# Expert weight tables: one product a token in place of two, the other one-hots from another engine

## The reference

```
e1 = jnp.take_along_axis(i1, ci // K, axis=-1)
e2 = jnp.take_along_axis(i2, ci % K, axis=-1)
idx = e1 * PEER_NKEYS + e2
g = jax.nn.softmax(sc, axis=-1)
...
a = jnp.einsum('cd,chkd->chk', xc, u[ic])
act = (jax.nn.gelu(a.astype(jnp.float32)) * gc).astype(xc.dtype)
return jnp.einsum('chk,chkd->cd', act, v[ic])
```

## Time and profile before

| | us |
|---|---|
| median of 3 runs | 4493.68 (4482.83 to 4499.79) |
| the profiled execution | 4483.95 |
| its span | 4482.2 |
| stage `expert_weights`, steps with quads (64) | about 1234 to 1702 |
| the same stage, steps without (16) | about 1702 to 1793 |

### The profile page before, as it was taken

One profiled execution on the slowest core, in us unless ns is written; L12 is line 12 of the kernel. 1 busy time (PEld: TensorE's weight loads), 2 busy tenths in 40 slices (PEclk: granted clock), 3 DMA queues, 4 the chain that ended last, 5 costly groups with the idle time before them and its releaser, 6 DMA issues. The chain is left out here.

```text
span 4482.2 us, 49622 instructions
## 1 busy us (share of the span) xinstructions
PE 4152.0 (93%) x18593; PEld 3324.3 (74%) x18600; DVE 2397.5 (53%) x4975; ACT 1390.3 (31%) x2104; POOL 107.2 (2%) x84
## 2 busy tenths in 40 slices
PE   6987888699999999899999999898999899898998
PEld 5863676478888888788888776676888667776886
DVE  3236345559999993454444444565442444565443
ACT  2222233223344443232222232243222232243221
POOL 0003000000000000000000000100000001000000
PEclk8987878899999999999999998999999999999999
DMA  2214000233444444666666322232223222242222
GB/s 99 98 44 78 1 1 17 69 104 136 143 145 183 184 186 171 196 190 189 193 189 191 102 83 68 73 128 83 94 92 92 75 73 78 67 143 76 94 90 71
DMA packets 188675, 491.87 MB, mean 110 GB/s; under 512 B 19554, under 2 KB 61956, under 8 KB 187300
## 3 DMA queue, kind: packets, MB, share of 16 engines
q1 hardware_dynamic: 188452, 488.88, 33.8%
HBM read 407.02 MB, written 81.79 MB: 109 GB/s over the span
## 5 line engine op out<-in xcount | busy, mean ns | idle before, releaser
L1016 DVE TENSOR_TENSOR stream_lo<-stream_raw,stream_hi 128x1024 fp32r<-128x1024 f32 (+1 forms) x538 | 653.4, 1215 | 750.7 <-ACT stream_hi L1008 749.2
L1008 ACT ACTIVATE stream_hi<-stream_raw 128x1024 fp32r<-128x1024 f32 (+1 forms) x538 | 563.1, 1047 | 1269.0 <-PE experts_ps L1464 492.1
L1464 PE MATMUL experts_ps<-outputs_a_hi,stream_hi 128*128 128x512 f32 x1024 | 404.6, 395 | 14.3 <-DVE outputs_a_lo L1434 14.3
L1045 PE MATMUL experts_ps<-h_hi,stream_hi 128*128 128x512 f32 x1024 | 406.7, 397 | 5.9 <-DVE stream_lo L1016 4.4
L1045 PE MATMUL experts_ps<-h_lo,stream_hi 128*128 128x512 f32 x1024 | 402.6, 393 | 0.0
L1464 PE MATMUL experts_ps<-outputs_a_hi,stream_lo 128*128 128x512 f32 x1024 | 402.2, 393 | 0.0
L1045 PE MATMUL experts_ps<-h_hi,stream_lo 128*128 128x512 f32 x1024 | 400.0, 391 | 0.0
L1464 PE MATMUL experts_ps<-outputs_a_lo,stream_hi 128*128 128x512 f32 x1024 | 398.3, 389 | 0.0
L2341 PE MATMUL ffn_ps<-h_hi,stream_hi 128*128 128x512 f32 x704 | 287.6, 408 | 25.3 <-DVE h_lo L2378 25.3
L2341 PE MATMUL mid_ps<-h_hi,stream_hi 128*128 128x512 f32 x672 | 288.2, 429 | 23.8 <-DVE h_lo L2378 20.8
L2342 PE MATMUL ffn_ps<-h_lo,stream_hi 128*128 128x512 f32 x704 | 279.6, 397 | 0.0
(11 more groups left out here) (437 smaller groups left out, 7713.8 us busy)
## 6 DMA issues: line engine op xcount, KB each, us to landing
stream_raw<-u SPq DMA_DIRECT2D x128, 512.0 KB, 3.4
stream_raw<-v SPq DMA_DIRECT2D x128, 512.0 KB, 4.0
stream_raw<-l_gu SPq DMA_DIRECT2D x88, 512.0 KB, 3.2
expert_hidden<-experts_gelu SPq DMA_DIRECT2D x128, 256.0 KB, 2.3
expert_weights<-weights_built SPq DMA_DIRECT2D x8, 4096.0 KB, 14.5
outputs_wgt<-expert_weights SPq DMA_DIRECT2D x32, 1024.0 KB, 7.9
outputs_a_raw<-expert_hidden SPq DMA_DIRECT2D x128, 256.0 KB, 4.2
stream_raw<-l_gate SPq DMA_DIRECT2D x48, 512.0 KB, 3.6
```

The source lines that it names most:

```text
L1008: self.nc.scalar.activation(self.hi[n % self.RING][:, 0:w], self.raw[n % self.RAW][:, 0:w], ACT.Copy).then_inc(self.hi_done, 1)
L1016: self.nc.vector.tensor_tensor(self.lo[n % self.RING][:, 0:w], self.raw[n % self.RAW][:, 0:w], self.hi[n % self.RING][:, 0:w].bitcast(F32) ...
L1045: mm = self.nc.tensor.matmul(self.ps[n % 2], a, b[:, k, :], start=(k == 0 and m == 0), stop=(k == DC - 1 and m == 2))
L1464: mm = nc.tensor.matmul(ps[d], v, a[b % RING][:, :], start=(b == 0 and m == 0), stop=(b == KEYS - 1 and m == 2))
```

## The change

The roles of the three tiles are swapped. The one-hot of e1 is now plain, and ScalarE makes it: four instructions Abs(iota - e1) of 128 columns and one Relu(1 - x) of 512 columns in place, a quad (`ones`, `hot1`); `minus` holds -e1. The one-hot of e2 carries the weight, and VectorE makes both halves, times the rounded g and times its rest, in one scalar_tensor_tensor of 256 columns a token (`weighted`, `hot2`); g has rounded value and rest side by side. TensorE does one product of 256 columns a token, the e1 tile stationary, and so the two halves arrive in PSUM side by side and are not added there. VectorE adds them on the way out, in one tensor_reduce a quad that reads 1024 values a partition, a pair being 128 words apart, and writes 512 (`take`). A quad fills two PSUM banks, so three places take six banks. The 128 quads are spread over 72 of the 80 steps, one or two a step.

```
--- before.py
+++ after.py
@@ -1261,69 +1261,87 @@
-    QUAD, RING, BANKS, BUILT = 4, 3, 4, 2
+    QUAD, RING, PLACES, BUILT = 4, 3, 3, 2
     N = SEQ // QUAD
     TILE = WT // QUAD
     first, last = CHOICE_STEPS, KEYS
-    PER = 2
+    SPREAD = last - first - 8
     with Stage(nc, name) as st:
-        g_hi, g_lo = st.sb("g_hi", [P, SEQ], F32R), st.sb("g_lo", [P, SEQ])
-        hot = [st.sb(f"hot{b}", [P, QUAD, 3, KEYS], F32R) for b in range(RING)]
+        g, minus = st.sb("g", [P, SEQ, 2], F32R), st.sb("minus", [P, SEQ])
+        hot1 = [st.sb(f"hot1_{b}", [P, QUAD, KEYS], F32R) for b in range(RING)]
+        hot2 = [st.sb(f"hot2_{b}", [P, QUAD, 2, KEYS], F32R) for b in range(RING)]
         built = [st.sb(f"built{b}", [P, KEYS, WT]) for b in range(BUILT)]
-        g_hi_done, g_lo_done, hot_done, mm_done, taken = (
-            st.sem(x) for x in ("g_hi_done", "g_lo_done", "hot_done", "mm_done", "taken"))
+        minus_done, g_hi_done, g_lo_done, far_done, hot1_done, hot2_done, mm_done, taken = (
+            st.sem(x) for x in ("minus_done", "g_hi_done", "g_lo_done", "far_done", "hot1_done", "hot2_done", "mm_done", "taken"))
         stored = [st.sem(f"stored{b}") for b in range(BUILT)]
         def quads(n):
-            return range(max(0, min(N, PER * (n - first))), max(0, min(N, PER * (n - first + 1))))
+            done = [N * max(0, min(SPREAD, step)) // SPREAD for step in (n - first, n - first + 1)]
+            return range(*done)
+        def place(quad):
+            return ps[:, 1024 * (quad % PLACES):1024 * (quad % PLACES) + 1024].rearrange("p (t s e) -> p t s e", t=QUAD, s=2)
         with nc.Block() as block:
             @block.scalar
             def _(act):
-                nc.scalar.activation(g_hi[:, :], chosen[:, 2, :], ACT.Copy).then_inc(g_hi_done, 1)
-                def take(quad):
-                    tt = quad // TILE
-                    if tt >= BUILT and quad % TILE == 0:
-                        act.wait_ge(stored[tt % BUILT], 16 * (tt // BUILT))
-                    act.wait_ge(mm_done, quad + 1)
-                    at = quad % TILE * QUAD
-                    nc.scalar.activation(built[tt % BUILT][:, :, at:at + QUAD].rearrange("p e t -> p t e"),
-                                         ps[quad % BANKS].rearrange("p (t e) -> p t e", t=QUAD),
-                                         ACT.Copy).then_inc(taken, 1)
+                nc.scalar.activation(minus[:, :], chosen[:, 0, :], ACT.Copy, scale=-1.0).then_inc(minus_done, 1)
+                nc.scalar.activation(g[:, :, 0], chosen[:, 2, :], ACT.Copy).then_inc(g_hi_done, 1)
+                act.wait_ge(minus_done, 1)
+                def ones(quad):
+                    if quad >= RING:
+                        act.wait_ge(mm_done, quad - RING + 1)
+                    to = hot1[quad % RING]
+                    for k in range(QUAD):
+                        t = quad * QUAD + k
+                        ins = nc.scalar.activation(to[:, k, :], C.iota, ACT.Abs, bias=minus[:, t:t + 1])
+                    ins.then_inc(far_done, 1)
+                    act.wait_ge(far_done, quad + 1)
+                    nc.scalar.activation(flat(to[:, :, :]), flat(to[:, :, :]).bitcast(F32), ACT.Relu, bias=C.ones[:, 0:1],
+                                         scale=-1.0).then_inc(hot1_done, 1)
                 for n in range(first, last):
                     hidden.activate(act, n - 1)
                     chunks.high(act, n + AHEAD)
+                    for quad in quads(n):
+                        ones(quad)
+                hidden.activate(act, last - 1)
+            @block.vector
+            def _(dve):
+                V = nc.vector
+                dve.wait_ge(g_hi_done, 1)
+                V.tensor_tensor(g[:, :, 1], chosen[:, 2, :], g[:, :, 0].bitcast(F32), ALU.subtract).then_inc(g_lo_done, 1)
+                dve.wait_ge(g_lo_done, 1)
+                def weighted(quad):
+                    if quad >= RING:
+                        dve.wait_ge(mm_done, quad - RING + 1)
+                    both = [P, 2, KEYS]
+                    for k in range(QUAD):
+                        t = quad * QUAD + k
+                        ins = V.scalar_tensor_tensor(out=hot2[quad % RING][:, k, :, :], in0=C.iota.unsqueeze(1).to_broadcast(both),
+                                                     scalar=chosen[:, 1, t:t + 1],
+                                                     in1=g[:, t, :].bitcast(F32).unsqueeze(2).to_broadcast(both),
+                                                     op0=ALU.is_equal, op1=ALU.mult)
+                    ins.then_inc(hot2_done, 1)
+                def take(quad):
+                    tt, at = quad // TILE, quad % TILE * QUAD
+                    if tt >= BUILT and quad % TILE == 0:
+                        dve.wait_ge(stored[tt % BUILT], 16 * (tt // BUILT))
+                    dve.wait_ge(mm_done, quad + 1)
+                    V.tensor_reduce(built[tt % BUILT][:, :, at:at + QUAD].rearrange("p e t -> p t e"),
+                                    place(quad).rearrange("p t s e -> p t e s"), AX_X, ALU.add).then_inc(taken, 1)
+                for n in range(first, last):
                     for quad in quads(n - 1):
                         take(quad)
-                hidden.activate(act, last - 1)
-            @block.vector
-            def _(dve):
-                dve.wait_ge(g_hi_done, 1)
-                nc.vector.tensor_tensor(g_lo[:, :], chosen[:, 2, :], g_hi[:, :].bitcast(F32),
-                                        ALU.subtract).then_inc(g_lo_done, 1)
-                dve.wait_ge(g_lo_done, 1)
-                def ones(quad):
-                    if quad >= RING:
-                        dve.wait_ge(mm_done, quad - RING + 1)
-                    for k in range(QUAD):
-                        t = quad * QUAD + k
-                        key1, key2 = chosen[:, 0, t:t + 1], chosen[:, 1, t:t + 1]
-                        V = nc.vector
-                        V.tensor_scalar(hot[quad % RING][:, k, 0, :], C.iota, key1, g_hi[:, t:t + 1].bitcast(F32),
-                                        ALU.is_equal, ALU.mult)
-                        V.tensor_scalar(hot[quad % RING][:, k, 1, :], C.iota, key1, g_lo[:, t:t + 1],
-                                        ALU.is_equal, ALU.mult)
-                        ins = V.tensor_scalar(hot[quad % RING][:, k, 2, :], C.iota, key2, None, ALU.is_equal)
-                    ins.then_inc(hot_done, 1)
-                for n in range(first, last):
                     for quad in quads(n):
-                        ones(quad)
+                        weighted(quad)
                     chunks.low(dve, n + AHEAD)
             @block.tensor
@@ -1331,13 +1349,13 @@
                 for n in range(first, last):
                     hidden.product(pe, n)
                     for quad in quads(n):
-                        pe.wait_ge(hot_done, quad + 1)
-                        if quad >= BANKS:
-                            pe.wait_ge(taken, quad - BANKS + 1)
+                        pe.wait_ge(hot1_done, quad + 1)
+                        pe.wait_ge(hot2_done, quad + 1)
+                        if quad >= PLACES:
+                            pe.wait_ge(taken, quad - PLACES + 1)
                         for k in range(QUAD):
-                            out, of = ps[quad % BANKS][:, k * KEYS:(k + 1) * KEYS], hot[quad % RING]
-                            nc.tensor.matmul(out, of[:, k, 0, :], of[:, k, 2, :], start=True, stop=False)
-                            mm = nc.tensor.matmul(out, of[:, k, 1, :], of[:, k, 2, :], start=False, stop=True)
+                            mm = nc.tensor.matmul(place(quad)[:, k, :, :], hot1[quad % RING][:, k, :], hot2[quad % RING][:, k, :, :],
+                                                  start=True, stop=True)
                         mm.then_inc(mm_done, 1)
             @block.sync
@@ -2332,7 +2350,7 @@
                     hidden.ps = bank[0:2]
                     expert_choice(nc, "choice", C, q, A["subkeys"], chosen, chunks, hidden,
                                   ps[:, 1024:3072].rearrange("p (h k) -> p h k", k=KEYS), bank[6])
-                expert_weights(nc, "weights", C, chosen, w_dram, chunks, hidden, bank[2:6])
+                expert_weights(nc, "weights", C, chosen, w_dram, chunks, hidden, ps[:, 1024:4096])
             expert_outputs(nc, "outputs", x, w_dram, a_dram, chunks, bank, C2, A["positions"], constants2)
```

More of the change, by code:

```diff
@@ L1298, in _ @@
                     chunks.high(act, n + AHEAD)
-                    for quad in quads(n - 1):
-                        take(quad)
+                    for quad in quads(n):
+                        ones(quad)
                 hidden.activate(act, last - 1)
@@ L1324, in _ @@
                 for n in range(first, last):
+                    for quad in quads(n - 1):
+                        take(quad)
                     for quad in quads(n):
-                        ones(quad)
+                        weighted(quad)
```

## The result

| | before | after |
|---|---|---|
| median, first comparison (4 runs each) | 4488.26 (4481.43 to 4499.79) | 4427.6 (4424.89 to 4429.25) |
| ratio, with its 95% interval | | 0.9862 (0.9837 to 0.9886) |
| the profiled execution | 4483.95 | 4427.55 |
| its span | 4482.2 | 4425.8 |
| gelu of step 48 to gelu of step 127 | 549.84 | 495.24 |

A forecast was written before the change was run, and what follows sets the result against it. TensorE was taken as the bound, VectorE close behind. TensorE's -47.6 us plus 2 us of stalls, -46, took the profiled 4483.95 to 4438; the 9.7 us median offset made 4448, range of 8 in 10 4434 to 4510.

The forecast's parts named there:

- A: VectorE's `take`: paired reads 128 words apart cost a hop on each read, take 2.19 us, +53 us, 4547; chance 0.17.
- B: VectorE's `take`: the hop falls on the writes alone and is not hidden, take 1.67 us, -13 us, 4481; chance 0.12.
- rival D: ScalarE's quads cost over 2.8 us through a longer wait before the Relu; at 3.2, 4496; chance 0.05.
- Rival C: TensorE: a 256-column product isn't cheaper than two of 128, 0.216 us each, +0.5 us, 4494; chance 0.04.
- of the 1.811 us of a burst 16 x 0.108 = 1.73 are its products, 0.08 is for entering and leaving it: TensorE's burst of 16 small products in a step; the fixed 0.08 us over 72 bursts adds 5.8 us.
- 0.122: TensorE: predicted us for one 256-column product, 0.107 + 0.016; 512 of them make 62.5 us.
- the 2 us of small stalls: Allowance for small stalls in the stage, because `take` stands ahead of `weighted` on VectorE with 0.8 us slack.
- 68.3 + 2: Stage's predicted us for products and bursts on TensorE, 62.5 + 5.8 = 68.3, plus 2 for small stalls.
- the median of the runs lay 9.7 us above that execution, so for a median I say 4448: Whole time: carries the 9.7 us between earlier median and profiled execution over, from 4438 to 4448.
- The own range of the forecast: Whole time 4439 to 4465 us, from product price 0.108 to 0.148 and stalls 0 to 5; chance 0.62.
- the wider range: The whole time's range of 8 in 10, 4434 to 4510 us, up to a mild read hop, take 1.9.
- the lower end of the stage's term: TensorE's saving in the stage if a 256-column product costs the load alone, 0.108 us: -55 us.

## Why the prediction was right and where it was wrong

**What bounds.** Right: TensorE before and after, VectorE just behind. Both kernels that pushed VectorE's step over TensorE's, one by 0.1 us a step (two quads in every step) and one by 1.7 (plain one-hots on VectorE, 8.13 in most two-quad steps), turned the bound over.

**VectorE.** Right to two hundredths: `weighted` 0.395, `take` 1.13 for 1.15, `low` 1.14. Rivals A and B fell with the 1219 ns of the reduce. The pair, 128 words apart in PSUM, is read at the rate of contiguous reduces, 1024 x 1.04 + 0.15 = 1.21, and the scattered writes are hidden, which the run with two products shows by their price alone. The Trainium skill, "Vector Engine (DVE) Microarchitecture Reference", SBUF access granule, has the full rate for a one-source operation that alternates between two regions, 16 KiB apart there; the trace agrees with that statement, and shows it for PSUM.

**ScalarE.** Right: a quad costs 1.93 for 2.0, far from the 2.81 at which rival D begins.

**TensorE.** The mechanism was right in what the rows can show: the stationary tile that comes with each product sets the price, and 256 columns beside it are nearly free. Rival C fell (0.120, not 0.216). Two sizes were off, both in the TensorE part:

- *The step "of the 1.811 us of a burst 16 x 0.108 = 1.73 are its products, 0.08 is for entering and leaving it" failed.* It took the price of a product from starts inside a burst and gave the rest to the burst as a fixed price, 72 x 0.08 = 5.8 us of the sum. The spread of before over 72 steps (under 0.02 a burst) and the two orders with 128 columns show that there is no price of that size. Of the 1.811, 0.01 is the first step's wait, shared out over the 63 steps that were averaged; the other 1.80 belongs to the products: 1.80 / 16 = 0.113, which is the 0.113 that an extra product of 128 columns costs.
- The product was 0.120 and not 0.122, which is 1 us.

With the 2 us of small stalls that did not come, these make the 9 us by which the stage was overrated: the steps of the stage hold 495.24 - 79 x 5.493 = 61.3 for the products, where the prediction had 68.3 + 2.

(The Trainium skill, "TensorE: Matmul & The Clock Gate", LDWEIGHTS, puts a load at its columns / 1.2, so 107 ns for 128. The extra product of 64 columns, at 0.110, stands as near to that as rows can tell.)

**The execution and the median.** *The step "the median of the runs lay 9.7 us above that execution, so for a median I say 4448" failed too,* and it is the largest part of the miss. It carried the distance between the three runs' median and one execution over to the changed kernel. But the median of 20 later runs of the kernel before is 4479.1, 4.9 *below* it, and the changed kernel's median and its profiled execution agree (4427.6 and 4427.55). Three runs between 4482.83 and 4499.79 did not fix a median to 10 us. The miss of 4448 - 4427.6 = 20.4 is then 9.7 from this, 9.0 from the stage's sum (TensorE and the stalls), and 1.9 from the start of the stage, to rounding.

**The range.** The own range of the forecast, 4439 to 4465, rested on the product's price and on stalls alone. Its lower end took -55 for the stage, and the stage gave -54.6: for the stage alone the measurement lies just inside. What put the time below 4439, and below the 4434 of the wider range, is the 9.7 and the 1.9. The scatter of the time ahead of the stage, and of the median that the sum was carried to, were not in the range, and they are as large as the term in dispute. That the lower end of the stage's term came so close is luck in its parts: 512 x 0.108 + 5.8 = 61.1 is nearly the measured 61.3 = 512 x 0.120, with a product too cheap and a burst's price that is not there.

## What to carry to other kernels

Count loads and not columns: here every matmul brought its own load, even of the tile that was there already, and up to 256 columns are almost free beside one. So put what shares the tile side by side in one product and let the engine that empties PSUM add it. Take the price of a small operation from whole periods (steps with it and without, divided by its count) and not from start to start inside a burst, and do not make a fixed price out of what is left over. Before you let another engine take over work, add up its whole step: 0.1 us a step over TensorE's cost 6.5 us here, and stayed invisible in the busy share.

## What the runs showed of the hardware that was not expected

- Prices of a float32r product with its load of a 128 x 128 stationary tile, at full clock and by whole steps: 0.110 (64 columns), 0.113 (128), 0.112 (192), 0.120 (256), 0.229 (512). A second product on the same tile costs as much as one on another tile (549.28 in both kernels).
- VectorE writing 512 values 64 words apart takes 1086 ns where the contiguous copy takes 691; ScalarE had 1117 against 597. Under a reduce of pairs none of it shows.
- With 64 steps, `weighted` has a median duration of 573 ns and the reduce of 1315, against 478 and 1218 in the kernel after, but the distances between starts are the same (0.396 and 1.13). Durations stretched where VectorE never waited; why is open.
- The code ahead of the stage is the same in all twelve profiled executions, and the stage starts up to 13 us apart (1231.4 to 1244.7). In the window from 550 to 750, in an attention stage, the granted clock (third number from the end) is 0.75 in the run with two products of 128, whose profiled execution took 4486.72, and 0.80 in the kernel after:

```profile
550.00:750.00 200.00, 175.47 (x925) 143.30 (x926) 96.15 (x324) 63.82 (x249) 0.51 (x2) 0.75 0.00 1
```
```profile
550.00:750.00 200.00, 174.37 (x976) 144.04 (x975) 97.58 (x328) 65.61 (x254) 0.52 (x2) 0.80 0.00 1
```

From the first to the last reduce of that stage's `nsa_top` these two took 188.0 and 178.9 us. Over all twelve the mean clock of that stretch and its length go together, from 188.0 at 0.76 to 178.7 at 0.81. It is one part of the scatter only: these two starts of the stage differ by 4.6 and not by 9.1. What decides which clock an execution gets was not tried.
